# Second feed-forward output of a two-layer transformer kernel by seven products of 128-token halves, with three quarters of its weight sums on GpSimd

## The reference, cut to what matters

```python
f = conv_ffn(modulate(h_lat, sh2, sc2), ffn_w_in[i], ffn_conv_w[i], ffn_conv_b[i], ffn_w_out[i])
h_lat = layer_norm(DEEPNORM_ALPHA * h_lat + g2 * f, ln2_g[i], ln2_b[i])
...
def conv_ffn(h, w_in, conv_w, conv_b, w_out):
    u = h @ w_in                       # 1024 -> 5632
    ...                                # depthwise convolution over 3 positions
    a, g = jnp.split(u, 2, axis=-1)
    return (jax.nn.silu(g) * a) @ w_out    # 2816 -> 1024
```

## Time and profile before

| | |
|---|---|
| median of three runs | 1872.05 us |
| profiled execution, first to last instruction (span) | 1869.9 us |
| TensorE busy, share of the span | 1722.4 us, 92% |
| VectorE busy | 921.5 us, 49% |
| ScalarE busy | 373.2 us, 20% |
| GpSimd busy | 0.2 us, 0% |
| mean granted TensorE clock | 0.968 |
| stage of `ffn_out1`, TensorE's first to last matmul of L699 | 1066.9 to 1144.9 us |

### The profile page before, as it was taken

How to read it: one execution, slowest core, us unless ns; L and a number is a source line. 1 busy time by engine, 2 the same in 40 slices (tenths; PEclk the granted TensorE clock), 3 DMA queues, 4 the chain that set the end, 5 groups by cost and what they waited for, 6 DMA issues and landing times.

```text
span 1869.9 us, 33176 instructions
## 1 busy us (share of the span) xinstructions
PE 1722.4 (92%) x14060; PEld 1360.1 (73%) x14060; DVE 921.5 (49%) x1988; ACT 373.2 (20%) x893; POOL 0.2 (0%) x4
## 2 busy tenths in 40 slices
PE   7999999999999999999999999999999767667776
PEld 4565687888888886776888888888888555545554
DVE  1488879666667428787544412577433111111112
ACT  0343413211110014222211102213402000000001
POOL 0000000000000000000000000000000000000000
PEclk9999999999999999999999999999999988888888
DMA  9524342222231214553334633331297999999997
GB/s 385 209 114 154 132 167 90 90 76 74 81 140 45 101 47 190 206 193 157 129 142 144 249 125 136 136 127 77 96 383 306 426 427 429 428 428 429 428 427 311
DMA packets 36161, 394.20 MB, mean 211 GB/s; under 512 B 3936, under 2 KB 7264, under 8 KB 14816
## 3 DMA queue, kind: packets, MB, share of 16 engines
q1 hardware_dynamic: 36064, 392.79, 52.2%
HBM read 391.72 MB, written 1.05 MB: 210 GB/s over the span
## 4 chain that ended last, share of the span: by engine, by line
PE 79%; DMA 19%; DVE 1%; issue 1%; ACT 0%; SPq 0%; DVEq 0%
PE bank L645 20%; DMA ring<-w_moe 18%; PE bank L1936 14%; PE bank L1643 9%; PE bank L699 5%; PE bank L2195 3%; PE bank L2241 3%; PE bank L3760 2%; PE bank L944 2%; PE bank L3515 2%; PE bank L2191 1%; PE bank L1249 1%; PE bank L3749 1%; PE bank L853 1%; PE bank L2839 1%; PE bank L1234 1%
## 5 line engine op out<-in xcount | busy, mean ns | idle before, releaser
L645 PE MATMUL bank<-layer_input,ring 128*128 128x256 f32 x1136 | 249.6, 380 | 0.0
L645 PEld LDWEIGHTS bank<-layer_input,ring 128*128 128x128 f32 x1136 | 214.9, 190 | 30.7 <-issue 2.7
L3749 PE MATMUL bank<-arena 128*32 128x128 f32 x2008 | 77.9, 320 | 51.4 <-DMA arena<-w_moe 49.3
L1643 PE MATMUL bank<-arena,ring 128*128 128x256 f32 x544 | 121.7, 380 | 0.0
L3901 DVE TENSOR_TENSOR arena<-arena,bank 128x128 f32<-128x128 f32 x32 | 9.2, 288 | 217.9 <-PE bank L3749 217.9
L1936 PE MATMUL bank<-arena 128*128 128x256 f32 x504 | 115.7, 380 | 0.0
L1643 PEld LDWEIGHTS bank<-arena,ring 128*128 128x128 f32 x544 | 103.4, 190 | 14.1 <-issue 0.4
L3749 PEld LDWEIGHTS bank<-arena 128*32 128x32 f32 x2008 | 67.2, 130 | 62.6 <-DMA arena<-w_moe 58.8
L1936 PEld LDWEIGHTS bank<-arena 128*128 128x128 f32 x504 | 95.9, 190 | 12.9 <-DVE arena L2065 0.2
L699 PE MATMUL bank<-arena,ring 128*128 128x256 f32 x444 | 97.0, 380 | 0.0
L3749 PE MATMUL bank<-ring,arena 128*32 128x128 f32 x1920 | 66.1, 296 | 28.9 <-DMA ring<-w_moe 28.8
(11 more groups left out here) (526 smaller groups left out, 2733.0 us busy)
## 6 DMA issues: line engine op xcount, KB each, us to landing
arena<-w_moe SPq DMA_DIRECT2D x45, 2048.0 KB, 25.8
ring<-w_moe SPq DMA_DIRECT2D x45, 2048.0 KB, 26.5
ring<-w_ffn_in SPq DMA_DIRECT2D x22, 2048.0 KB, 7.7
ring<-w_proj SPq DMA_DIRECT2D x7, 3072.0 KB, 10.0
ring<-w_ada_late SPq DMA_DIRECT2D x8, 2560.0 KB, 9.3
ring<-w_ffn_out SPq DMA_DIRECT2D x7, 2816.0 KB, 10.0
ring<-w_na_pair SPq DMA_DIRECT2D x5, 2048.0 KB, 7.7
arena<-w_far SPq DMA_DIRECT2D x16, 512.0 KB, 4.8
```

What stands on the lines that cost most here:

```text
L645: last = pe.matmul(out, a, b, start=(k == 0), stop=(k == len(lhs) - 1))
L1643: last = eng.matmul(out, w[:, k * P:(k + 1) * P], x[:, k, :], start=(start and k == 0), stop=(stop and k == half - 1), skip_group_check=True)
L3749: ins = eng.matmul(bank[x][group[q], 0:P], xe[:, k, SLOTS * e:SLOTS * e + SLOTS], weight(e, first, last, (x * KT + k) * FE + q * P, P), st ...
```

## The change

The second layer's output product is done by `split_out` as well, with 128-token halves and hidden halves of 11 tiles, which leaves no tile over. `split_out` gets parameters for its width, places and gains; what the first layer and the attention output need beside it moves to `split_layer`. The weights of the output are laid out in pairs of output tiles, four chunks of 5632 columns. Three of them go through the ring, and the chunk of pair 1 goes to `self.N`, which is why the load of `cmp` (the next stage's, also in `self.N`) moves behind pair 1. With one chunk less in the ring, the slots of all later loads change places, and so do the two ends of the ring that `branch` and `w_out` use and the order of two parts of expert 1. The weight sums of pair 0 stay on VectorE; those of pairs 1 to 3 get a program on GpSimd. Two families of semaphores (`open_in`, `far_in`) are merged into `rows_in`.

```diff
-          ("ffn_in1", 11, 4096), ("ffn_out1", 4, 5632),
+          ("ffn_in1", 11, 4096), ("ffn_out1", 3, 5632),
...
+HALF_LAST = FT // 2
+LAST_STEPS = split_steps(FT, FT, False)
+LAST_IN_RING = (0, 2, 3)
+LAST_FAR = 1
...
-    "ffn_in1": ("ffn1_up_done", each(2)), "ffn_out1": ("y_ready", each(2, RESIDUAL_BASE["ffn_out1"])),
+    "ffn_in1": ("ffn1_up_done", each(2)), "ffn_out1": ("ffn1_up_done", lambda j: LAST_STEPS[1][LAST_IN_RING[j], SEVEN]),
...
+    def pool_program(self, pool):
+
+        done, summed = self.sem("ffn1_up_done"), self.sem("pool_summed")
+        half, g0 = HALF_LAST * P, FIRST["ffn_out1"]
+        s1 = self.extra[:, 0:half]
+        for c in range(1, 4):
+            if c == LAST_FAR:
+                slot = self.last_far()
+                pool.wait_ge(self.sem("second_in"), 32 + 16)
+            else:
+                g = g0 + LAST_IN_RING.index(c)
+                slot = self.ring[g % 2]
+                pool.wait_ge(self.w_loaded[g % 2], 16 * (g // 2 + 1))
+            w11, w12, w21, w22 = [slot[:, i * half:(i + 1) * half] for i in range(4)]
+            at = 4 * (c - 1)
+            pool.wait_ge(done, LAST_STEPS[1][c - 1, 3])
+            if c == 1:
+                pool.wait_ge(self.sem("ffn1_link"), 2 * FT + 5)
+            else:
+                pool.wait_ge(summed, at - 1)
+            pool.tensor_tensor(s1, w21, w22, ALU.add).then_inc(summed, 1)
+            pool.wait_ge(summed, at + 1)
+            pool.tensor_tensor(w21, w11, w21, ALU.subtract).then_inc(summed, 1)
+            pool.wait_ge(done, LAST_STEPS[1][c, 1])
+            pool.wait_ge(summed, at + 2)
+            pool.tensor_tensor(w11, s1, w11, ALU.subtract).then_inc(summed, 1)
+            pool.wait_ge(done, LAST_STEPS[1][c, 2])
+            pool.wait_ge(summed, at + 3)
+            pool.tensor_tensor(w12, w12, w11, ALU.subtract).then_inc(summed, 1)
...
             if name == "ffn_out1":
 
-                sp.wait_ge(self.sem("ffn1_up_done"), 1)
+                sp.wait_ge(self.sem("na_biased"), 4 * NA_PAIRS)
+                sp.dma_start(self.last_far(), self.W["ffn_out1_b"][0]).then_inc(self.sem("second_in"), 16)
+            if name == "proj":
+
+                sp.wait_ge(self.sem("ffn1_up_done"), LAST_STEPS[1][LAST_FAR, SEVEN])
                 sp.dma_start(self.mix_views()["cmp_w"], self.W["cmp"][0]).then_inc(self.sem("cmp_in"), 16)
...
         def places(c):
-            two = bank[1 + 5 * (c % 2)]
-            return bank[5 * (c % 2)][:, 0:256], two[:, 0:256], two[:, 256:512], bank[o["last"] if c == 3 else 7][:, 0:256]
+            e = (c + o["turn"]) % 2
+            two = bank[1 + 5 * e]
+            return bank[5 * e][:, 0:m], two[:, 0:m], two[:, m:w], bank[o["last"] if c == 3 else 7][:, 0:m]
...
                 if i == 3:
-                    eng.wait_ge(s["sums_ready"], ready + (1 if c else 2))
+                    eng.wait_ge(summed(c), ready + (1 if c else 2))
...
             def early_sums(c, count):
+                if c and pooled:
+                    return
...
-        self.residual_norm(who, eng, "ffn_out1", rhs, FT, 2, 5, 1, (1,), lambda k: self.A[:, k, CTX:T], g, b,
-                           write_input, sources)
+        holes = self.hidden[:, :, LAT:T]
+        near, far = slice(0, HALF_LAST), slice(HALF_LAST, FT)
+        ffn = {"up_done": self.sem("ffn1_up_done"), "snapped": self.sem("ffn1_gate_out"),
+               "sums_ready": self.sem("ffn1_link"), "up_used": self.sem("ffn1_up_used")}
+        self.split_out(who, eng, ffn, dict(
+            name="ffn_out1", source=self.hidden[:, :, 0:LAT], half=HALF_LAST, nk=FT, steps=LAST_STEPS, sums=2 * FT, used=FT,
+            per=1, gate=5, layer=1, segs=(1, 1), width=LAT, sum_at=0, last=7, turn=1, gain=g, bias=b,
+            chunk=LAST_IN_RING.index, far=self.last_far(), squares=[self.A[:, k, CTX:T] for k in range(KT)],
+            between=lambda part: self.fill(eng, (2, 1, 6)[part], self.bank[1]),
+            token_sums=[holes[:, near, 0:P], holes[:, far, 0:P], holes[:, near, P:LAT]],
+            spare=[self.X[:, 3072 + P * i:3072 + P * (i + 1)] for i in range(5)], write_input=write_input,
+            arrived=lambda part: eng.wait_ge(self.sem("ffn1_hid_done"), (HALF_LAST, FT)[part])))
```

More of the change, by code:

```diff
@@ L295, in _ @@
                 self.run("dve", dve)
+            @block.gpsimd
+            def _(pool):
+                self.pool_program(pool)
             @block.sync
@@ L499, in load_opening @@
         sp.dma_start(self.V[:, 2 * KT:EARLY_V], self.vec_d[:, 2 * KT:EARLY_V]).then_inc(self.const_in, 16)
-        arrived = [self.sem(f"open_in{g}") for g in range(4)]
+        arrived = [self.sem(f"rows_in{g}") for g in range(4)]
         landed = (arrived[0], self.w_loaded[0], self.w_loaded[1], arrived[2], arrived[3])
@@ L1566, in ffn @@
                     eng.activation(sg[e], u[e][1], ACT.Silu).then_inc(gate_out, 1)
[L1568 to L1573, removed]
+        self.hidden = hid
     def ffn_split(self, who, eng):
@@ L1591, in ffn_split, with split_layer, write_input, split_out @@
             arrived=lambda part: eng.wait_ge(s["hid_done"], hid[part])))
-    def split_out(self, who, eng, s, o):
+    def split_layer(self, who, eng, s, o):
         g, b = [self.vec(f"ln{o['ln']}_{x}", 0, KT) for x in "gb"]
         ga, ba = self.next_gains(who, eng, g, b, *o["to"])
+        self.a_base = self.claim(who, a_ready=KT)["a_ready"]
+        half, spare = o["half"], o["spare"]
+        def write_input(k, x):
+            for seg in range(2):
+                c = slice(CTX * seg, CTX * seg + CTX)
+                to, of = self.A[:, k, c], x[:, c]
+                if o["by_columns"] and seg:
+                    to, of = to.rearrange("p (c r) -> p r c", r=GRID_H), of.rearrange("p (r c) -> p r c", r=GRID_H)
+                last = eng.activation(to, of, ACT.Identity, bias=ba[:, k, seg:seg + 1], scale=ga[:, k, seg:seg + 1])
+            last.then_inc(self.sem("mix_a_ready"), 1)
+        sums = [self.N[:, i * 2560:i * 2560 + half * 256].rearrange("p (k t) -> p k t", k=half) for i in range(3)]
+        places = [spare[0][:, 0:256], spare[0][:, 256:512], spare[1][:, 0:256], spare[1][:, 256:512], self.N[:, 7680:7936]]
+        self.split_out(who, eng, s, o | dict(gain=g, bias=b, width=T, layer=0, segs=(0, 1), token_sums=sums, spare=places,
+                                             chunk=lambda c: c // o["per"], turn=0, write_input=write_input))
+    def split_out(self, who, eng, s, o):
+        g, b, w = o["gain"], o["bias"], o["width"]
+        c0, m, q = T - w, w // 2, w // 4
         order, done, snaps, snapped = o["steps"]
         half, nk, squares, per = o["half"], o["nk"], o["squares"], o["per"]
-        self.a_base = self.claim(who, a_ready=KT)["a_ready"]
         names = ("mean_ready", "centred", "squared", "var_ready", "dev_ready", "rstd_ready", "rstd_spread", "normed")
@@ L1650, in rest @@
                     o = (x * nk + k) * P
-                    last = eng.matmul(out, slot[:, o:o + P], src[:, k, col:col + 256], start=(start and k == 2 * half),
+                    last = eng.matmul(out, slot[:, o:o + P], src[:, k, col:col + m], start=(start and k == 2 * half),
                                       stop=(k == nk - 1), skip_group_check=True)
@@ L1691, in step @@
                     eng.wait_ge(s["up_used"], used_0 + c)
-                    last = rest(d, c, 1, CTX, start=True)
+                    last = rest(d, c, 1, m, start=True)
                 if i == 7 and nk > 2 * half:
                     eng.wait_ge(s["snapped"], snapped[c, 6])
-                    eng.wait_ge(s["sums_ready"], ready + (4 if c else 8))
+                    eng.wait_ge(summed(c), ready + (4 if c else 8))
                     product(a, w22, t4, False)
@@ L1722, in spread @@
                 for j in range(4):
-                    last = eng.matmul(b[:, j * P:(j + 1) * P], self.con("spread", j * P, P), src, start=True, stop=True,
+                    last = eng.matmul(b[:, j * q:(j + 1) * q], self.con("spread", j * P, P), src, start=True, stop=True,
                                       skip_group_check=True)
```

113 lines of the change are left out of this document (62 added, 51 removed).

## The result

The changed kernel takes 1878.17 us (median of 7 runs, 1877.17 to 1878.83) against 1872.05 for the kernel before (7 runs, 1871.72 to 1873.83). The ratio is 1.0029 with a 95% interval of 1.0018 to 1.0039: slower, by about 6 us, where the forecast was 1865.3. The time lies inside the stated range of 1863.5 to 1879 only because that range was stretched to take in the slower rival; the forecast's own range ended at 1868. The profiled execution spans 1876.8 us against 1869.9, so the comparison of traces explains 6.9 us. It is 0.2% to 0.4% of a kernel, and all of it has to be found in one stage of 91 us.

What follows compares the result with a forecast made beforehand. TensorE bounds the stage, by matmul records times their distance. -7.65 + 0.65 + 0.1 + 0.25 - 0.14 = -6.8 us gives span 1863.1 and, with 2.15 us between span and median, 1865.3 us; range 1863.5 to 1879.

Steps and rivals of the forecast that it cites:

- Twelve sums of 1408 elements: GpSimd's weight sums for pairs 1 to 3: free as long as each is there when its product is.
- Matmuls, saved 7.65 us: Output product on TensorE: 616 records of 128 columns at 111.3 ns replace 352 of 256 at 216 ns.
- The start, 0.65 us and up to 0.1: Stage start: (1,1) loses 0.65 us behind the last convolution, (0,4) up to 0.1 for VectorE's fifth sum.
- GpSimd's sum, 3.2 us as a guess: One weight sum on GpSimd, taken as twice VectorE's 1.62 us; bounds 1.62 and 8.9 us.
- The limit of 3.67 us: Pairs 1 to 3: each GpSimd sum must take less, semaphores included, to be there for its product.
- VectorE's new work, "all hidden": Pair 0: eight VectorE sums of 1.62 us, ending at 1084.7, hidden behind products, nothing to spare at (0,4).
- its combining, "some 0.3 us each": VectorE, per pair: about ten operations of 128 columns, hidden against 17.2 us per pair.
- Loads, nothing: Moved weight chunks, `cmp` and `proj`: none late by less than 10 us, no bytes moved, no cost.
- The sum of -6.8 us: All terms of the stage together: it ends near 1138.1 instead of 1144.9, giving 1865.3 us.
- The row sums: Stage end: twelve groups instead of ten stand ahead of the end of (3,7), 0.25 us lost.
- A gain or loss passes through whole: Behind the stage: the DMA-saturated stretch starts earlier or later with the stage's end, its bytes unchanged.
- GpSimd and VectorE shut each other out: Slower rival: SBUF reads exclude each other in strict turns, (1,5) waits, 12.8 us later, 1878; chance 0.28.

Runs made afterwards that it cites:

- GpSimd early: All weight sums on VectorE and scaling moved behind the residual steps, plus GpSimd making pair 0's first two sums and (1,1) waiting for one step less: 1865.19 us.
- GpSimd starting later: Changed kernel with GpSimd's first sum held back until VectorE has made all eight sums of pair 0: 1879.52 us, ratio 1.0034.
- the floor: Changed kernel without the weight sums of pairs 1 to 3, TensorE's waits on them or a GpSimd program: 1865.81 us, stage 77.61 us.
- the shortened wait: Product (1,1) waits for 21 up-projection release steps, not 22; made together with GpSimd's two early sums of pair 0 (1865.19 us), not run alone.

## Why the prediction was wrong

The step that failed is the one on GpSimd: "Twelve sums of 1408 elements. They cost nothing as long as each is there when its product is." They were there, and cost 13 us. Point by point:

- **Matmuls, saved 7.65 us: the distance right, the saving 0.6 us too large (see the sum below).** 111.6 ns per small record over 88 of them, against 111.3 from 16.
- **The start, 0.65 us and up to 0.1: right.** (1,1) starts 3.16 us behind (0,1) in the changed kernel, where a product takes 2.46: 0.7 us, of which the bracket shows 0.55. (0,4) is on time.
- **GpSimd's sum, 3.2 us as a guess: right, and of no use.** Undisturbed ones take 3.15 to 3.24 us. By the ratio in the Trainium skill, GPSIMD Engine Reference, section Performance versus the Vector engine, it was 3.2; here it is 3.17 / 1.62 = 1.96, and the trace agrees. The limit of 3.67 us was kept on the engine's own speed, but three sums that had VectorE's between them took 4.14 to 4.42 us. I had bounded how long GpSimd takes, and not what else takes longer meanwhile.
- **VectorE's new work, "all hidden", and its combining, "some 0.3 us each": failed.** Held steps took about 3 us each. The seventh and eighth sums ended at 1089.02, 23.5 us into the stage; the forecast's 84.7 less its start at 1066.9 is 17.8.
- **Loads, nothing: right.** No product waits for a load. The chunk in the fixed place took longer to land than I had said (14.3 us against 9.9), with room to spare:

```profile
arena<-w_ffn_out_b SPq DMA_DIRECT2D x1, 2816.0 KB, 14.3
```

- **The sum of -6.8 us: right as a floor.** Without the sums the stage is 6.04 us shorter. Of the missing 0.8 us, some 0.2 is the distance of the records (616 x 0.3 ns). About 0.5 is in gaps where TensorE passes between products and row sums: in that trace the last three products take 7.56 us, from 1131.09 to 1138.65, where 66 records at 111.6 ns make 7.37. The row sums themselves cost 0.1 more than I had put.
- **A gain or loss passes through whole: right within about 2 us.** The next stage starts 5.6 us later and the span is 6.9 longer; with GpSimd early, 8.4 earlier and 7.1 shorter; with GpSimd starting later, 7.2 later and 9.2 longer. From the first matmul of the next stage to the end of the execution the ten traces take 719.4 to 721.4 us, and the kernel before lies at one end of that. So each trace has some 2 us of its own outside the stage, whose cause I haven't found; it is why the stage was compared by its length.

The rival "GpSimd and VectorE shut each other out" had 0.28 and named 1878. Its mechanism is right in place and order: turns of whole instructions, short waits ahead of (0,6) and (0,7), and the large one at (1,5) behind ScalarE's copy, itself behind `far_rows`. Its size came out right by two errors that cancel, which is luck. It put 12.8 us on the delay of (1,5). I read the delay by the distance between starts, since the brackets count from a record's modelled end and so leave out some 0.2 us of each wait. From (0,4) to (1,3) TensorE takes 13.10 us instead of the 9.82 of the floor, and from (1,4) to (1,5) 9.73 instead of 2.46: 3.28 + 7.27 = 10.55. `far_rows` ended 38.0 us into the stage instead of 40.2. 1.5 us of that is in the turns, which were a little shorter than I had priced them: the sixth GpSimd sum ended 36.3 us into the stage and not 37.8. The other 0.7 is that four operations were left behind it and not seven, as not all that I had queued are held: those that read a bank in PSUM took 0.29 us (L1899) with a GpSimd sum running. Another such place, VectorE and then GpSimd:

```profile
1119.23 1.42 DVE L1928 SCALAR_TENSOR_TENSOR arena<-bank,residual 128x256 f32<-128x256 f32 x4 [4.47 <-PE bank L1807]
```

```profile
1119.69 3.18 POOL L350 TENSOR_TENSOR ring<-ring 128x1408 f32<-128x1408 f32 x1
```

What I had not foreseen at all gave the difference back: after 7.1 us without work TensorE was granted 0.50 for 4 us, and the three products from (1,5) on took 9.80 us from start to start instead of 7.37 at the floor's distance, 2.43 us. The same 66 records took 10.28 and 10.40 us after waits of 6.98 and 7.80 us, against 9.97 here and 7.63 without such a wait. 10.55 + 2.43 = 12.98 us is all by which this stage is longer than the floor (90.59 - 77.61).

The choice of the forecast is the fault behind all this. The row for GpSimd had nothing but a fill of one element, and I wrote "No row here can agree or disagree" of the one rule that spoke against the change, then gave more to the case that needs the rule not to hold (0.46 against 0.28 + 0.15). By the prediction's own count six operations with two operands in SBUF stood in exactly that stretch; the rival's turns could be worked out to the microsecond, and were. Where the rows are silent on a resource that two engines share, silence is no evidence for independence.

## What to carry to other kernels

Work moved to GpSimd isn't taken off VectorE if both read SBUF: each VectorE operation with two SBUF operands, and each `tensor_scalar`, may cost one whole GpSimd instruction, about 3 us here for a step of 0.3. Before moving it, list what VectorE has queued in that stretch, and give GpSimd only the stretches in which TensorE's slack exceeds one such hold, or where VectorE has none. Look for the loss in the durations of VectorE's small operations and in "issue" in the chain, since no wait is shown for it; and add to a wait of some 7 us on TensorE the matmuls at half the clock that follow, 2.4 us here. When two edits are made together, ask the trace which of them gave the gain: here the shortened wait gave 0.78 us and GpSimd's early sums at most 0.15.

## What the runs showed of the hardware

- The hold by kind of operation, the first four with a GpSimd sum running: `tensor_tensor` of two SBUF operands, 8.97 us for two instead of 3.29; `scalar_tensor_tensor` of SBUF operands, 5.78 for two instead of 0.61; `tensor_scalar`, 3.34 for two instead of 0.49 (3.14 for the first, 0.28 for the second); with one operand in a PSUM bank, 0.29, not held. With a fill running: `tensor_tensor` not held, `tensor_scalar` 3.17 for two instead of 0.49; `scalar_tensor_tensor` of SBUF operands was not seen beside one.
- It goes both ways: GpSimd's sums took 4.14, 4.42 and 4.37 us where VectorE's sums stood between them, and 3.15 to 3.24 otherwise. In the stretch above neither engine got two instructions in a row while the other had one ready that needs the same.
- TensorE's granted clock was 0.50 from 1103.9 to 1107.9 after 7.2 us with 0.17 us of work, and 0.92 on average over the 5.7 us behind that.
